# Moving three activation tiles by 384 or 256 bytes against their weight tiles, in a one-core block of recurrent, attention and feed-forward layers

## The chip, the cores and the metric

One NeuronCore of a Trainium2 chip runs the whole program. The metric is the device time of one execution in microseconds. For the kernel before, three runs gave 1909.07, 1909.23 and 1911.52 us, a median of 1909.23 us.

## What is computed

A batch of one sequence with 256 tokens and 1024 channels goes through two blocks. All tensors are float32. The first block has a recurrent layer, a gated feed-forward network, an attention layer and a second network; the second block has two modulated layers, each of which feeds one large projection into three branches (attention, a delta-rule recurrence, a gated linear attention) and merges them.

```
def swiglu_layer(x, norm_g, w_gate_up, w_down):
    h = rmsnorm(x, norm_g)
    g, u = jnp.split(h @ w_gate_up, 2, axis=-1)
    return x + (jax.nn.silu(g) * u) @ w_down

def second_block(...):
    for l in range(DEPTH):
        h = _rms_norm(x, norm_pre[l]) * (1 + scale[:, None, :]) + shift[:, None, :]
        p = h @ w_in[l]
        ...
        merged = (jax.nn.sigmoid(gate_a) * o_mla + jax.nn.sigmoid(gate_b) * o_rwkv
                  + jax.nn.sigmoid(gate_c) * o_gla)
        y = merged @ w_out[l]
        x = x + gate[:, None, :] * _rms_norm(y, norm_post[l])
```

What matters here are the products of activations with large weight matrices: `h @ w_in`, `h @ w_gate_up`, the product with `w_down`, the projections to queries, keys and values, and the output projections.

## The kernel before

Channels lie on the 128 partitions and tokens along the free axis (T = 256), so a tensor of 1024 channels is a tile of 8 rows (`DK`) of 256 float32 in each partition, 1024 bytes a row.

A large product is made in three passes. Weights and activations are each split into a rounded part (type float32r) and the rounded rest; the product is the sum of high by high, high by low and low by high. Each pass over 128 channels is one matmul that streams 256 columns, with a weight load of 128 columns ahead of it. Such a matmul, rounded, 128 by 256, is called a rounded matmul below; the program has 11,112 of them, and some fp32 matmuls between them.

Weights come in units of 1024 x 128 (`UNIT`, 4096 bytes in a partition). SyncE loads one into one of five raw slots (`UNIT_RAW`), ScalarE (L726) or VectorE (L721) writes its high part into one of three slots (`UNIT_HIGH`), and VectorE writes the low part over the raw one (`UNIT_LOW`, L737). TensorE then works through the unit with 24 rounded matmuls: in `multiply_unit` (L712, where the weights are the loaded operand and the activation streams; L701, the `by_token` form, where the activation is the loaded operand and the weights stream) or, for the first two units of a layer, in `first_units_by_pieces` (L671). The activation is `HX`, the layer's input, in most of these products; it is `H_PARTS` in the projections to queries, keys and values, and another tile (`DIRECT_HIGH`, `OM_HIGH`, `R_HIGH`, `OG_HIGH`, `M_HIGH` and others) in the output projections.

The feed-forward networks (`ffn_pe`, with `three_passes` at L1490, L1491 and L1492, and L1505 for the first piece) work in the same way with `H_PARTS` as the input of the up projection and `HIDDEN_PARTS`, the inner rows, as that of the down projection. Their weight parts are in `part_slots`. The up projection is a loop over 11 turns of two halves, 48 rounded matmuls a half; the down projection a loop over 4 turns of two halves, 66 rounded matmuls a half. Here ScalarE (L2396, L2428) and VectorE (L2316, L2324) split the weights, and VectorE evicts and gates the results (L2329 to L2346; L2346 writes the low part of the inner rows).

All tiles stand at addresses that are written out by hand. All weight tiles of these products begin at the same byte modulo 512, their rows are 512 or 1024 bytes, and those of the activations 1024. So the distance from a matmul's weight operand to its streamed operand, modulo 512, is the same for every matmul of a product. `LINE` (128 floats, 512 bytes) is the room in which a tile is shifted, and `X_SHIFT`, `H_SHIFT` and `HIDDEN_SHIFT` (L185) give the shift of the high and low tile in floats:

```
X_SHIFT, H_SHIFT, HIDDEN_SHIFT = (16, 16), (16, 16), (48, 48)
HX = [shaped(x_room[:, X_SHIFT[e] + e * DK * T:X_SHIFT[e] + (e + 1) * DK * T], (DK, T)) for e in range(2)]
om_at += (lent + X_SHIFT[0] - om_at) % 64
```

The first line is L185, the second L338, the third L390: `OM_HIGH` and `OM_LOW`, which feed one output projection in each layer of the second block, follow `X_SHIFT`, but modulo 64 floats (256 bytes).

The order of the work is the order in which it is written for each engine, with semaphores between the engines; no scheduler has a hand in it.

Of the kernel before, what the change touches and what calls it, by code (L numbers as in the profile page):

```python
# [163 lines left out]
def program(nc, A, out, stop=None):  # L164
    with ExitStack() as ctx:
# [16 lines left out]
        KD_ = FFN // P  # L182
        UNIT, RAWS, HIGHS = DK * P, 5, 3
        LINE = 128
        X_SHIFT, H_SHIFT, HIDDEN_SHIFT = (16, 16), (16, 16), (48, 48)  # L185
        WHOLE = 2 * KD_ * COLS + 2 * 2 * T + LINE
        SPLIT_AT, SPLIT = COMMON + WHOLE, 2 * 2 * DK * COLS + 2 * DK * T + 2 * KD_ * T + 2 * LINE
        psum = [ctx.enter_context(nc.psum_tensor(f"bank{i}", [P, 512], F32))[:, :] for i in range(8)]
# [3778 lines left out]
```

How the kernel before makes its waits and increments, by code:

```python
        def load_first_up(l):  # L564
            sp.wait_ge(unit_used.sem, last_split[l] + 1)
            for s in range(2):
                for to, frm in ffn_up[l].loads(s, WHOLE_UP[s]):
                    sp.dma_start(to, frm).then_inc(landed[s].sem, 16)
# [1 line left out]
        def load_up(l):  # L571
            job, turns = ffn_up[l], turns_before[l]
            with sp.Fori(1, UPS) as j:
                for s in range(2):
                    sp.wait_ge(lo_ready[s].sem, j + turns)
                    for to, frm in job.loads(j * 2 + s, WHOLE_UP[s]):
                        sp.dma_start(to, frm).then_inc(landed[s].sem, 16)
# [1 line left out]
        def load_down(l):  # L579
            job, turns = ffn_down[l], turns_before[l]
            for q in range(2):
                sp.wait_ge(lo_ready[q].sem, turns + UPS)
                for to, frm in job.loads(q, WHOLE_DOWN[q]):
                    sp.dma_start(to, frm).then_inc(landed[q].sem, 16)
            with sp.Fori(1, DK // 2) as j:
                for q in range(2):
                    sp.wait_ge(lo_ready[1].sem, j * 2 + (turns + UPS + q - 1))
                    for to, frm in job.loads(j * 2 + q, WHOLE_DOWN[q]):
                        sp.dma_start(to, frm).then_inc(landed[q].sem, 16)
# [46 lines left out]
        def load_units(job):  # L636
# [1 line left out]
                u = job.first + i  # L638
                if u >= RAWS:
                    sp.wait_ge(unit_used.sem, u - RAWS + 1)
                for to, frm in job.loads(i, UNIT_RAW[u % RAWS].rearrange("p (k c) -> p k c", k=job.kt)):
```

## Time and profile before

| | |
|---|---|
| median of three runs | 1909.23 us |
| the profiled execution, its own time | 1910.01 us |
| its span on the core | 1908.2 us |
| TensorE matmul busy | 1829.3 us, 96% |
| TensorE weight load busy | 1719.4 us, 90% |
| VectorE busy | 1367.7 us, 72% |
| ScalarE busy | 852.7 us, 45% |
| granted TensorE clock, mean | 0.992 |
| moved by DMA | 291.97 MB, 153 GB/s |

Busy time counts a matmul from its start to its modelled end, some 280 ns, while the next one begins some 115 ns after it: matmuls overlap in the pipeline. The pace is the distance from one start to the next. The profile's chain of waits, which goes back from the last instruction to what released each step, counts a matmul only until the next one starts, and so a merged piece of the chain (start, time, line, count) gives the pace as time divided by count.

### The profile page before, as it was taken

Reading aid. Unit: us, or ns where it says so; the run is one execution under the profiler, and the core shown is the slowest. Engines: PE = TensorE matmul, PEld = TensorE weight load, DVE = VectorE, ACT = ScalarE, POOL = GpSimd, SP = SyncE. Lnnn points to the kernel's source line nnn. Section 1 sums busy time; section 2 is a strip of 40 time slices with the busy share of each in tenths; the row PEclk is TensorE's granted clock in tenths of the full one; section 3 lists DMA queues with packets and bytes.
Section 4 is the critical chain, followed back from the end, with each engine's and each line's share of the span. In section 5 each row is a group of like instructions: output and inputs, shape, how many; then the busy total and the mean of one; then the engine's idle time right before and its main releaser. Section 6 shows DMA issues by size and latency. Waiting matters only on the chain.

```text
span 1908.2 us, 43158 instructions
## 1 busy us (share of the span) xinstructions
PE 1829.3 (96%) x18639; PEld 1719.4 (90%) x18639; DVE 1367.7 (72%) x1735; ACT 852.7 (45%) x1263; POOL 88.3 (5%) x131
## 2 busy tenths in 40 slices
PE   7999999999899999999998999997999998999999
PEld 7987999998699999998997899997998997889988
DVE  8996688758748876776886469666776886458755
ACT  5572534345634333226764233254216774334154
POOL 2000000010500000002000000000002000000000
PEclk9999999999999999999999999999999999999999
DMA  8555477975437795663560145554663561145544
GB/s 226 146 144 155 122 243 261 272 204 161 117 100 248 263 275 139 163 181 92 160 172 4 54 117 166 144 150 127 156 183 94 155 172 32 38 110 158 164 123 132
DMA packets 473230, 291.97 MB, mean 153 GB/s; under 512 B 26775, under 2 KB 467580, under 8 KB 472872
## 3 DMA queue, kind: packets, MB, share of 16 engines
q1 hardware_dynamic: 466720, 262.13, 48.6%
q0 software_dynamic: 5312, 25.32, 3.5%
q10 hardware_dynamic: 1032, 2.11, 0.4%
q8 instruction: 128, 2.10, 0.4%
q14 instruction: 38, 0.31, 0.0%
HBM read 287.95 MB, written 1.05 MB: 151 GB/s over the span
## 4 chain that ended last, share of the span: by engine, by line
PE 80%; DVE 12%; ACT 4%; issue 2%; DMA 2%; ACTq 0%; DVEq 0%; POOL 0%; SPq 0%
PE bank L712 39%; PE bank L1490 6%; PE bank L1491 6%; PE bank L1492 6%; DVE rounded L737 3%; PE bank L953 3%; PE bank L671 3%; PE bank L701 2%; PE bank L1678 1%; PE bank L1691 1%; PE bank L945 1%; DVE rounded L721 1%; ACT rounded L726 1%; PE bank L1659 1%; PE bank L794 1%
## 5 line engine op out<-in xcount | busy, mean ns | idle before, releaser
L712 PE MATMUL bank<-rounded 128*128 128x256 f32 x6504 | 789.9, 282 | 12.2 <-DVE rounded L737 9.9
L712 PEld LDWEIGHTS bank<-rounded 128*128 128x128 f32 x6504 | 771.0, 188 | 27.3 <-DVE rounded L737 14.5
L737 DVE TENSOR_TENSOR rounded<-arena,rounded 128x1024 fp32r<-128x1024 f32 x331 | 400.2, 1216 | 87.1 <-ACT rounded L726 78.1
L726 ACT ACTIVATE rounded<-arena 128x1024 fp32r<-128x1024 f32 x216 | 227.1, 1058 | 163.2 <-PE bank L712 108.6
L1490 PE MATMUL bank<-parts 128*128 128x256 f32 x1024 | 286.7, 280 | 2.3 <-DVE parts L2324 2.3
L1491 PE MATMUL bank<-parts 128*128 128x256 f32 x1024 | 285.4, 279 | 0.0
L1492 PE MATMUL bank<-parts 128*128 128x256 f32 x1024 | 285.2, 279 | 0.0
L1490 PEld LDWEIGHTS bank<-parts 128*128 128x128 f32 x1024 | 192.7, 188 | 3.5 <-issue 1.6
L1492 PEld LDWEIGHTS bank<-parts 128*128 128x128 f32 x1024 | 192.2, 188 | 0.0
L1491 PEld LDWEIGHTS bank<-parts 128*128 128x128 f32 x1024 | 191.9, 187 | 0.1
L777 ACT ACTIVATE arena<-bank 128x512 f32<-128x512 f32 x90 | 53.2, 596 | 238.6 <-PE bank L712 227.0
L2396 ACT ACTIVATE parts<-whole 128x2048 fp32r<-128x2048 f32 x44 | 84.3, 1917 | 127.4 <-PE bank L1492 104.1
L721 DVE CAST rounded<-arena 128x1024 fp32r<-128x1024 f32 (+1 forms) x115 | 78.2, 680 | 67.0 <-PE bank L712 41.9
L2316 DVE TENSOR_TENSOR parts<-whole,parts 128x2048 fp32r<-128x2048 f32 x44 | 100.8, 2292 | 19.2 <-ACT parts L2396 18.5
L953 PE MATMUL bank<-common,arena 128*128 128x128 f32 x519 | 77.8, 285 | 14.6 <-DMA common<-in_const 7.1
L953 PEld LDWEIGHTS bank<-common,arena 128*128 128x128 f32 x519 | 58.4, 144 | 25.0 <-DMA common<-in_const 7.1
L2324 DVE TENSOR_TENSOR parts<-whole,parts 128x1408 fp32r<-128x1408 f32 x32 | 52.0, 1625 | 36.5 <-ACT parts L2428 36.1
L2428 ACT ACTIVATE parts<-whole 128x1408 fp32r<-128x1408 f32 x32 | 44.2, 1381 | 66.2 <-PE bank L1492 52.9
L2713 DVE COPY arena<-bank 128x256 f32<-128x256 f32 (+2 forms) x64 | 33.6, 525 | 42.7 <-PE bank L1678 19.3
L712 PE MATMUL bank<-common,arena 128*128 128x256 f32 x256 | 59.8, 385 | 0.0
L701 PE MATMUL bank<-rounded 128*128 128x256 f32 x480 | 58.5, 282 | 0.7 <-DVE rounded L737 0.7
L701 PEld LDWEIGHTS bank<-rounded 128*128 128x128 f32 x480 | 56.6, 189 | 2.2 <-DVE rounded L737 1.1
(409 smaller groups left out, 2369.6 us busy)
## 6 DMA issues: line engine op xcount, KB each, us to landing
arena<-in_w_in SPq DMA_DIRECT2D x190, 512.0 KB, 3.8
whole<-in_ffn_w_gate_up SPq DMA_DIRECT2D x44, 1024.0 KB, 5.1
arena<-in_ada_w POOLq DMA_DIRECT2D x32, 768.0 KB, 6.3
whole<-in_ffn_w_down SPq DMA_DIRECT2D x16, 1408.0 KB, 6.9
arena<-in_rec_w_in SPq DMA_DIRECT2D x36, 512.0 KB, 3.7
arena<-in_att_w_qkv SPq DMA_DIRECT2D x24, 512.0 KB, 3.9
arena<-in_rec_w_out SPq DMA_DIRECT2D x16, 512.0 KB, 3.9
arena<-in_mla_w_o SPq DMA_DIRECT2D x16, 512.0 KB, 4.0
```

The lines of the kernel that those rows point to most:

```text
L671: last = pe.matmul(psum[s][:, i * T:i * T + T], w[a][:, kk, :], job.rhs[b][:, kk, :], start=(i, kk, a, b) == (0, 0, 0, 0), stop=kk == job. ...
L701: last = pe.matmul(psum[s][:, t * COLS:t * COLS + COLS], x[b][:, at + k, t * P:t * P + P], w[a][:, k, n * COLS:n * COLS + COLS], start=beg ...
L712: last = pe.matmul(psum[s][0:c, m % 2 * T:m % 2 * T + T], w[a][:, k, cols], x[b][:, k, :], start=(k, a, b) == (0, 0, 0), stop=k == job.kt ...
L721: write(high_view(job_of[u], u), raw_view(job_of[u], u, UNIT_RAW)).then_inc(done.sem, 1)
L726: high_parts(act, lambda to, frm: act.activation(to, frm, ACT.Copy), high_by_act[0].pop(0), unit_high_s)
L737: dve.tensor_tensor(raw_view(job_of[u], u, UNIT_LOW), raw, high_view(job_of[u], u).bitcast(F32), ALU.subtract)\
L953: last = pe.transpose(bank[:, n * P:n * P + P], x, ident)
L1490: pe.matmul(bank, w_hi, x_hi, start=start and k == 0, stop=False)
L1491: pe.matmul(bank, w_hi, x_lo, start=False, stop=False)
L1492: last = pe.matmul(bank, w_lo, x_hi, start=False, stop=stop and k == n - 1)
L2316: dve.tensor_tensor(UP_W[s][1], WHOLE_UP[s], UP_W[s][0].bitcast(F32), ALU.subtract)\
L2396: act.activation(UP_W[s][0], WHOLE_UP[s], ACT.Copy)\
```

## The change

One line is different. The three shifts become 112 floats, 448 bytes. No instruction is added, removed or moved on any engine; DMA transfers, waits and shapes are the same.

```diff
-        X_SHIFT, H_SHIFT, HIDDEN_SHIFT = (16, 16), (16, 16), (48, 48)
+        X_SHIFT, H_SHIFT, HIDDEN_SHIFT = (112, 112), (112, 112), (112, 112)
```

What this does to the distance of the streamed operand behind the weight operand, in bytes modulo 512, worked out from the addresses of all rounded matmuls:

| product | lines | before | after | rounded matmuls |
|---|---|---|---|---|
| `HX` and `H_PARTS` streamed | 671, 712 | 64 | 448 | 5,160 |
| up projections (`H_PARTS`) | 1490 to 1492, 1505 | 64 | 448 | 2,112 |
| down projections (`HIDDEN_PARTS`) | 1490 to 1492 | 192 | 448 | 1,056 |
| `HX` and `H_PARTS` as loaded operand | 701 | 448 | 64 | 576 |
| `OM_HIGH`, `OM_LOW` streamed | 712 | 320 | 192 | 384 |
| all others | 671, 701, 712 | 0 to 448 | the same | 1,824 |

In the fourth row the roles are exchanged, so a tile that begins 64 bytes behind the weights makes the weights begin 448 bytes behind it. The fifth row follows from the 256 bytes of L390. fp32 matmuls and the transposes keep their addresses.

## Rows read from the trace of the kernel before

**Rows 1.** The page, parts 1 and 2: busy time; granted TensorE clock by slice.
```profile
PE 1829.3 (96%) x18639; PEld 1719.4 (90%) x18639; DVE 1367.7 (72%) x1735; ACT 852.7 (45%) x1263; POOL 88.3 (5%) x131
PEclk9999999999999999999999999999999999999999
```
**Rows 2.** The page, part 4 (chain by engine), and the chain's shares by line.
```profile
PE 80%; DVE 12%; ACT 4%; issue 2%; DMA 2%; ACTq 0%; DVEq 0%; POOL 0%; SPq 0%
by line: PE bank L712 39.4%; PE bank L1490 6.0%; PE bank L1491 5.9%; PE bank L1492 5.8%; DVE rounded L737 2.9%; PE bank L953 2.6%; PE bank L671 2.5%; issue 2.2%; PE bank L701 2.1%; PE bank L1678 1.3%; PE bank L1691 1.2%; PE bank L945 1.1%;
```
**Rows 3.** Groups by form, PE: line, engine, operands, shape, count | busy us, mean ns | idle.
```profile
L712 PE MATMUL bank<-rounded 128*128 128x256 f32 x6432 | 781.7, 282 | 12.2 <-DVE rounded L737 9.9 <-ACT arena L777 1.6 <-ACT common L3323 0.6
L1490 PE MATMUL bank<-parts 128*128 128x256 f32 x1024 | 286.7, 280 | 2.3 <-DVE parts L2324 2.3
...
L701 PE MATMUL bank<-rounded 128*128 128x256 f32 x480 | 58.5, 282 | 0.7 <-DVE rounded L737 0.7
```
**Rows 4.** The chain in order of time, pieces of L712: start us, us, what, count.
```profile
943.43 31.09 PE bank L712 x264
...
1341.83 19.04 PE bank L712 x168
...
1386.43 42.41 PE bank L712 x360
```
**Rows 5.** Windows, all engines: two in up projections, the last in a down projection.
```profile
268.50:346.50 78.00, 78.00 (x664) 78.00 (x664) 64.96 (x56) 29.72 (x21) 3.70 (x7) 1.00 0.77 257
590.50:679.50 89.00, 89.00 (x758) 89.00 (x757) 74.09 (x64) 33.78 (x24) 4.23 (x8) 1.00 0.77 258
686.00:740.00 54.00, 54.00 (x479) 54.00 (x478) 36.87 (x31) 19.56 (x16) 2.11 (x4) 1.00 0.95 267
```
The columns of rows 5 are the stretch, its length, then busy time and count of PE, PEld, DVE, ACT and POOL, the granted clock, the busy share of the DMA engines and GB/s.

**Rows 6.** Timeline: the first and the last merged row of rounded matmuls.
```profile
18.15 0.84 PE L671 MATMUL bank<-rounded 128*128 128x256 f32 x5
...
1898.35 1.35 PE L712 MATMUL bank<-rounded 128*128 128x256 f32 x10
```
**Rows 7.** Windows, PE alone: L712 on OM_HIGH and OM_LOW.
```profile
912.00:933.00 21.00, 21.00 (x180) 1.00 0.61 174
```
**Rows 8.** The chain in order of time, pieces of L701.
```profile
853.33 2.75 PE bank L701 x24
859.77 2.75 PE bank L701 x24
...
1434.39 2.75 PE bank L701 x24
1440.82 2.83 PE bank L701 x24
```
**Rows 9.** Windows, PE alone: the three long stretches of L701.
```profile
472.00:487.00 15.00, 15.00 (x130) 1.00 0.30 88
1197.00:1206.00 9.00, 9.00 (x82) 1.00 0.70 184
1776.00:1786.00 10.00, 10.00 (x87) 1.00 0.67 179
```
**Rows 10.** Waits of PE: line, releaser, us in total, times, longest.
```profile
PE bank L712 <- DVE rounded L737: 10.6, 13, 1.4
```
**Rows 11.** The chain in order of time, in the first down projection.
```profile
359.35 10.15 DMA whole<-in_ffn_w_down
```
**Rows 12.** Groups by form, DVE: the two halves of a weight unit.
```profile
L737 DVE TENSOR_TENSOR rounded<-arena,rounded 128x1024 fp32r<-128x1024 f32 x328 | 399.3, 1224 | 87.0 <-ACT rounded L726 78.1
...
L721 DVE CAST rounded<-arena 128x1024 fp32r<-128x1024 f32 x112 | 77.5, 692 | 66.3 <-PE bank L712 41.2 <-PE bank L671 9.1 <-ACT arena L3859 8.6
```
**Rows 13.** Groups, DVE, from 590 to 680 us (an up projection).
```profile
L2346 DVE TENSOR_TENSOR parts<-apart,parts 128x512 fp32r<-128x512 f32 x8 | 5.6, 694 | 0.3
L2340 DVE TENSOR_TENSOR apart<-apart,common 128x512 f32<-128x512 f32 x8 | 5.5, 693 | 0.3
```

## The prediction

> **What bounds the kernel now.** I read first the page's shares: TensorE works in 1829.3 of 1908.2 us and its clock is granted in full in every slice, so it is on the upper of its two levels, 2.4 GHz, from end to end [rows 1]. Then the chain of waits: 80% of it is TensorE, and L712 alone is 39.4%, the three lines 1490 to 1492 another 17.7% [rows 2]. So what bounds the time is the pace at which one rounded 128x256 matmul follows another. The groups by form show nearly all of them in L712, L1490 to L1492 and L701, every one shown as some 280 ns long [rows 3]; that is the length of one in a pipeline and hides the pace. The pace stands in the chain's merged pieces, time divided by count. There the same instruction of the same line has two paces: 31.09 us / 264 = 117.8 ns and 42.41 / 360 = 117.8 ns, but 19.04 / 168 = 113.3 ns [rows 4]. Nothing released either, and the clock was the same. I take 4.5 ns as the price of the slow pace.
>
> The pace does not wander. A stretch keeps the one that it took within its first few matmuls, for as long as the stretch lasts: the windows of the feed-forward networks show it over 78 and 89 us (a window also counts the two or three matmuls that began just before it, so 89.00 / (758 - 2.5) = 117.8 ns), and over 54 us at the other pace (54.00 / (479 - 2.4) = 113.3 ns) [rows 5]. These two stretches also tell what the pace has to do with the change. They are the same three lines, the same loop body and the same weight tiles. The slow ones are the up projection, whose moving operand (H_PARTS) lies 64 bytes behind the weights modulo 512; the fast one is the down projection, whose moving operand (HIDDEN_PARTS) lies 192 bytes behind. The Trainium skill, TensorE: Matmul & The Clock Gate, Part 2, says in its step on LDWEIGHTS that weights and moving operand come through two independent read ports, so that loading weights takes nothing from a running matmul. This trace does not bear that out as it stands, with 113.3 beside 117.8 ns; what it would make of the change is the second rival.
>
> **What each place is worth, from the rows.** From the first rounded matmuls at 18.15 us to the last ten at 1898.35 there are 11,112 [rows 6]. Counted by the distance from one start to the next, with distances over 125 ns left out, the share at the fast pace is 13% of the 7,272 that go from 64 to 448, 68% of the 1,056 that go from 192 to 448 (57% of all that lie at 192), and none of the 384 of OM_HIGH, which go from 320 to 192 and run at 21.00 / (180 - 2.4) = 118 ns [rows 7].
>
> For 448 the trace has a stand-in. In L701 the layer's input is the weight operand and the weight tile streams, so there the moving operand lies 64 bytes ahead of the weights, which is 448 behind, modulo 512. Its separate pieces show both paces: 2.75 / 24 = 114.6 ns three times, which with a start of some 30 ns is the fast one, 2.83 / 24 = 118 ns for the slow one [rows 8]. Of three long stretches one is fast at 9.00 / (82 - 2.4) = 113.1 ns, and two are slow at 15.00 / (130 - 2.4) = 117.6 and 10.00 / (87 - 2.4) = 118.2 ns [rows 9]. That is 4 fast and 3 slow. Over all L701 matmuls at 448 it is 36%, because the longest stretch took the slow pace. The change swaps the two: 576 matmuls of L701 go from 448 to 64 (31% of these are fast now).
>
> **The sum.** No instruction, wait or transfer is added, removed or moved; only addresses change. Let p be the share at the fast pace at 448 after the change. The bounds of p are what the trace shows at the four places: none (320) and 68% (the down projection), and nothing excludes 100%, which the 54 us stretch reaches. Nearest is L701, with 36% by matmuls and 4 of 7 by stretches; starts at 192 look alike, with 57% by matmuls. What is short in L701 is long in L712, so I weight stretches more than matmuls and take p = 0.55.
>
> - 64 to 448: 7,272 x (0.55 - 0.13) = 3,054 more at the fast pace.
> - 192 to 448: 1,056 x (0.55 - 0.68) = 137 fewer.
> - 320 to 192: 384 x (0.57 - 0) = 219 more.
> - 448 to 64 in L701: 576 x (0.14 - 0.31) = 98 fewer (0.14 is the share over all 8,040 that lie at 64 now).
>
> Together 3,038 x 4.5 ns = 13.7 us of TensorE time. What of it reaches the end: L712 waits 10.6 us in all for the vector engine's halves of the weights [rows 10], some 1.4% of its time, and in the first down projection the chain runs through a 10.15 us load of weights [rows 11]. There a faster pace is lost in the wait behind it. I take 95%: 13.0 us. The cover elsewhere holds: a unit of 24 matmuls takes 24 x 117.8 = 2.83 us now and 2.72 then, against 1.22 us of L737 and 0.69 us of L721 on the vector engine, and in the up projection the vector engine is at 74.09 of 89.00 us, which becomes 87% [rows 5, 12]. Were that cover gone, the wait that comes next would be L712 on L737 again.
>
> The vector and scalar engines write the moved tiles. I cost that at nothing: L2346, which writes a moved tile, takes 694 ns and L2340, of the same shape with no such tile, 693 [rows 13]. A difference of a few ns would lie under the matmuls that these lines run beside.
>
> The profiled execution was 1910.0 us with a span of 1908.2; the median of the three runs is 1909.2, 0.8 us less. 1910.0 - 13.0 = 1897.0, against the median **1896 us**.
>
> Every tenth of p is worth (7,272 + 1,056) x 0.1 x 4.5 ns x 0.95 = 3.6 us, and the sum is zero at p = 0.185: there 7,272 x 0.055 = 400 and 219 are paid for by 523 in the down projections and 98 in L701. About 0.2%, or 3.8 us, is what a measurement of this kernel can tell from no change. So it is faster by more than that above p = 0.29 and slower by more than that below 0.08.
>
> **The rivals.**
>
> *The fast pace everywhere at 448* (p near 1). For it: the fast pieces of L701 lose some 30 ns in their first matmuls and then settle [rows 8], so a slow start at 448 need not last, and in a loop of hundreds there are many chances to slip. Against it: the 15 us in L701 that stayed slow from end to end [rows 9]. The time would be 1909.2 - 0.815 x 35.6 = 1880 us; at p = 0.9, 1884.
>
> *The place plays no part.* The paces would come from how each stretch happens to start, and each place in the program would keep its own. For it: L712 shows both paces at one and the same distance [rows 4]. Against it: 2,010 of 2,010 counted up-projection matmuls are slow and the second down projection is fast but for its beginning [rows 5], in the same lines. The time would be 1909. The page's two independent ports would make it come out so.
>
> *448 holds the slow pace.* At the start of the long stretches, the up projections above all, 448 lets the slow pace in as 64 and 320 do, and the down projections lose what 192 gave them. Place: L1490 to L1492 at 686 us and after. Price: with p = 0.05, (7,272 + 1,056) x (0.05 - 0.185) x 4.5 ns x 0.95 = 4.8 us, which is 1914 us. It decides below p = 0.185, and can be told from no change below 0.08. For it: of the three long stretches of L701 two are slow, the longest among them [rows 9], and the loops of the networks are longer still. Against it: four of all seven stretches at 448 are fast [rows 8, 9].
>
> *It does not do what it says.* OM_HIGH is aligned to 256 bytes and not to 512, so it lands at 192 and not 448; the term is in the sum, 0.9 us at most, and the forecast does not hang on it. That the remaining 1,824 matmuls, which keep their place, start in another phase can move the time by a microsecond either way.
>
> **How the numbers follow.** Chances: the forecast (p from 0.29 to 0.85) 0.60; fast everywhere 0.12; place plays no part, or p ends only just above its zero (0.185 to 0.29), 0.15; 448 holds the slow pace 0.13, of which 0.09 below p = 0.08. That gives faster 0.72, same 0.15 + 0.04 = 0.19, slower 0.09. The range runs from p = 0.9 (1884 us) to the point of no change (1909 us, p = 0.185), a little over both.
>
> **What would show it.** In the chain after, L712 pieces with 96 and more matmuls should mostly divide to 113 to 114 ns; in the windows of the up projections (89 us now) at least one should count about 113.3 ns a matmul and so end some 3 us sooner. The second down projection should be as fast as now, or slow at 117.8 ns and so some 2 us longer. L701's pieces should be slower, and L712 on OM_HIGH should show the fast pace in one of its two stretches. The forecast is wrong if all paces stand as before, if the up projections stay at 117.8 ns throughout, if a third pace shows up, or if matmuls get faster and the waits of L712 for L737 grow by as much.

## The result and the profile after

The changed kernel takes 1901.99 us in the median of 12 runs, the kernel before 1910.62 us in 12 runs beside it. The ratio is 0.9949, with a 95% interval of 0.9927 to 0.9971: faster by 0.5%, which is 9.7 us (the two medians lie 8.6 us apart). The profiled execution took 1903.7 us with a span of 1901.9, 6.3 us less than the profiled one of before.

The page after, busy time and the chain by engine, and below them the chain's shares by line:

```profile
PE 1820.5 (96%) x18639; PEld 1710.9 (90%) x18639; DVE 1366.7 (72%) x1735; ACT 852.7 (45%) x1263; POOL 88.6 (5%) x131
...
PE 74%; DVE 16%; ACT 5%; issue 3%; DMA 2%; ACTq 0%; DVEq 0%; POOL 0%; SPq 0%
```
```profile
by line: PE bank L712 34.7%; PE bank L1490 5.7%; PE bank L1491 5.6%; PE bank L1492 5.6%; DVE rounded L737 4.2%; issue 2.7%; PE bank L953 2.6%; PE bank L671 2.6%; PE bank L701 2.1%; DVE arena L1996 1.5%; ACT rounded L726 1.3%; PE bank L1678
```

The other engines' busy time is what it was. TensorE's share of the chain fell from 80 to 74%, L712's from 39.4 to 34.7%, and L737, which makes the low part of the weights, rose from 2.9 to 4.2% [rows 2]: a little of the path now runs through the vector engine. The chain in order of time, pieces of L712 after (start us, us, what, count):

```profile
757.93 19.04 PE bank L712 x168
...
940.22 31.09 PE bank L712 x264
...
1383.10 41.58 PE bank L712 x360
```

The first divides to 113.3 ns. The second is 117.8 ns to the digit, as in [rows 4] at 943.43. The third, 42.41 us before, is 115.5 ns: part of it changed pace, and the experiments below show which part. The windows of the networks, all engines: two in the first up projection, one in the second, and the second down projection last:

```profile
227.00:287.00 60.00, 60.00 (x512) 60.00 (x511) 47.26 (x42) 25.86 (x19) 2.65 (x5) 1.00 0.68 230
290.00:331.00 41.00, 41.00 (x364) 41.00 (x363) 35.08 (x30) 16.03 (x12) 2.12 (x4) 1.00 0.77 264
587.50:679.00 91.50, 91.50 (x779) 91.50 (x778) 75.51 (x67) 35.23 (x26) 4.24 (x8) 1.00 0.79 260
683.00:738.00 55.00, 55.00 (x469) 55.00 (x468) 36.02 (x30) 19.52 (x16) 2.12 (x4) 1.00 0.93 262
```

Less the 2.4 matmuls that began before a window, these are 117.7, 113.4, 117.8 and 117.9 ns. One stretch of the first up projection is fast; the second up projection is as slow as before, and the second down projection, fast in [rows 5], is now slow. OM_HIGH shows the fast pace in one of its two stretches (21.20 / 185.6 = 114.2 ns, and 118.2 ns), and of the four pieces of L701 in [rows 8] one stood at 2.83 us before and two do now:

```profile
908.80:930.00 21.20, 21.20 (x188) 1.00 0.64 181
1487.00:1508.00 21.00, 21.00 (x180) 1.00 0.63 175
```
```profile
852.41 2.75 PE bank L701 x24
858.85 2.83 PE bank L701 x24
...
1430.22 2.75 PE bank L701 x24
1436.66 2.83 PE bank L701 x24
```

Two covers that the prediction named: L712 waits 11.8 us for L737 in place of 10.6 [rows 10], and L2346, which writes a moved tile, keeps its 693 to 694 ns [rows 13].

```profile
PE bank L712 <- DVE rounded L737: 11.8, 16, 1.5
```

**Where the 6.3 us of the two profiles came from.** The time between starts, added up by product: the streamed layer input gave 7.1 us, the up projections 1.9, OM_HIGH 0.8 and the attention's projections 0.4; the down projections took 2.3, L701 0.8 and the unmoved products 0.8. The same time can be split by the length of the distances, each counted against 117.8 ns. Those up to 125 ns, which are the pace, gave 6.4 us. Of the longer ones, 25 fewer of the input's fell where the lower clock was granted, which gave 2.1 us. The others, at the full clock, are waits and breaks between products, and they took 2.1 us more than before.

### The profile page after: what moved, and what is told of

It reads as the page before. It is cut to its first block, busy times and chain, and to the rows that moved or that the text cites. A ratio compares the mean times of both kernels' runs of the same rounds, so it can differ in the third digit from the quotient of the medians.

```text
span 1901.9 us, 43158 instructions
## 1 busy us (share of the span) xinstructions
PE 1820.5 (96%) x18639; PEld 1710.9 (90%) x18639; DVE 1366.7 (72%) x1735; ACT 852.7 (45%) x1263; POOL 88.6 (5%) x131
## 4 chain that ended last, share of the span: by engine, by line
PE 74%; DVE 16%; ACT 5%; issue 3%; DMA 2%; ACTq 0%; DVEq 0%; POOL 0%; SPq 0%
PE bank L712 35%; PE bank L1490 6%; PE bank L1491 6%; PE bank L1492 6%; DVE rounded L737 4%; PE bank L953 3%; PE bank L671 3%; PE bank L701 2%; DVE arena L1996 1%; ACT rounded L726 1%; PE bank L1678 1%; PE bank L1691 1%; DVE rounded L721 1%; PE bank L945 1%; PE bank L1659 1%
## 5 line engine op out<-in xcount | busy, mean ns | idle before, releaser
L712 PE MATMUL bank<-rounded 128*128 128x256 f32 x6504 | 780.9, 281 | 13.4 <-DVE rounded L737 11.1
L712 PEld LDWEIGHTS bank<-rounded 128*128 128x128 f32 x6504 | 761.9, 188 | 28.9 <-DVE rounded L737 15.6
L737 DVE TENSOR_TENSOR rounded<-arena,rounded 128x1024 fp32r<-128x1024 f32 x331 | 399.8, 1216 | 85.1 <-ACT rounded L726 76.1
L712 PE MATMUL bank<-common,arena 128*128 128x256 f32 x256 | 59.8, 385 | 0.0
L701 PE MATMUL bank<-rounded 128*128 128x256 f32 x480 | 59.1, 282 | 0.6 <-DVE rounded L737 0.5
L701 PEld LDWEIGHTS bank<-rounded 128*128 128x128 f32 x480 | 57.1, 188 | 2.2 <-DVE rounded L737 1.2
```

The lines of the kernel that those rows point to most:

```text
L701: last = pe.matmul(psum[s][:, t * COLS:t * COLS + COLS], x[b][:, at + k, t * P:t * P + P], w[a][:, k, n * COLS:n * COLS + COLS], start=beg ...
L712: last = pe.matmul(psum[s][0:c, m % 2 * T:m % 2 * T + T], w[a][:, k, cols], x[b][:, k, :], start=(k, a, b) == (0, 0, 0), stop=k == job.kt ...
L737: dve.tensor_tensor(raw_view(job_of[u], u, UNIT_LOW), raw, high_view(job_of[u], u).bitcast(F32), ALU.subtract)\
```

## The experiments

The table gives for each profile the share at the fast pace, counted from one start to the next (up to 115 ns fast, 115 to 125 ns slow, longer distances left out). "Input" is the 4,776 matmuls of L671 and L712 that stream `HX`.

| kernel | distance of input, up, down | input | up | down | OM_HIGH |
|---|---|---|---|---|---|
| before | 64, 64, 192 | 20% | 0% | 68% | 0% |
| before again | 64, 64, 192 | 8% | 0% | 12% | 0% |
| after | 448, 448, 448 | 52% | 25% | 25% | 49% |
| after again | 448, 448, 448 | 63% | 7% | 71% | 1% |
| x_only | 448, 64, 192 | 58% | 0% | 77% | 1% |
| h_only | 64, 448, 192 | 20% | 4% | 80% | 0% |
| keep_hidden | 448, 448, 192 | 63% | 34% | 31% | 49% |
| all_192 | 192, 192, 192 | 48% | 2% | 24% | 37% |
| all_320 | 320, 320, 320 | 15% | 18% | 0% | 0% |
| all_128 | 128, 128, 128 | no such two paces | | | |
| all_224 | 224, 224, 224 | no such two paces | | | |
| fresh_448 | 448, 448, 448 | 55% | 87% | 52% | 1% |
| fresh_64 | 64, 64, 192 | 17% | 84% | 81% | 0% |
| two_distances | 192 and 448 | 67% | 2% | 40% | 1% |

**Both kernels a second time** (`before_again`, `after_again`), with no edit.

> The kernel before, unchanged, for a second profile. Theory (the distance between the operands sets how likely a stretch is to take the fast pace, and each stretch draws its pace anew in each execution): at 64 the draw is nearly always slow, so both up projections count 117.8 ns a matmul again, all 2,112 of them; at 192 it is mixed, so the down projections may come out otherwise than in the first profile, between 30% and 90% fast. Rival (the pace belongs to the place in the program and the way each stretch starts, the distance plays no part): the first down projection mixed and the second fast as in the first profile, stretch by stretch. Time within 0.3% of 1910 us under both.

> The changed kernel, unchanged, for a second profile. Theory: stretches at 448 draw anew, so several long stretches that were slow in the first profile are fast here and the other way about, with 35 to 60% of the 8,328 matmuls at 448 fast; the time lies anywhere between 1892 and 1912 us. Rival (pace belongs to the place): the same stretches fast and slow as in the first profile, and the time within 0.3% of the first profile's 1903.7 us.

Windows, PE alone, of the second profile of the kernel before (two up projections, then the second down projection), and of the second profile of the changed one in the same order; the columns are the stretch, its length, busy time and count, the granted clock, the DMA engines' busy share and GB/s:

```profile
230.00:330.00 100.00, 100.00 (x851) 1.00 0.72 242
580.00:680.00 100.00, 100.00 (x851) 1.00 0.78 261
695.00:745.00 50.00, 50.00 (x427) 1.00 0.95 268
```
```profile
235.00:345.00 110.00, 110.00 (x937) 1.00 0.77 257
580.00:670.00 90.00, 90.00 (x767) 1.00 0.75 257
698.00:750.00 52.00, 52.00 (x461) 1.00 0.98 274
```

Before: the up projections are at 100 / 848.6 = 117.8 ns again. The second down projection, 54 us at 113.3 ns in [rows 5], is at 50 / 424.6 = 117.8 ns, in the same kernel at the same place. After: the stretch of the first up projection that was fast is slow here, and the second down projection goes the other way, 117.9 to 113.4 ns.

So some stretches draw their pace anew in each execution, as the theory had it; the down projections' 12% lies below the 30% that was expected, and at 448 46% of the moved matmuls are fast, within the 35 to 60% expected. Others do not draw: the piece of L712 with 264 matmuls at 31.09 us (943.43 before, 940.22 after) takes 31.09 us in both second profiles too. The two times, 1921.1 and 1920.8 us, lie outside what was expected. Of the 11.0 us by which the span of the kernel before is longer than in its first profile, 3.4 lie between the starts of its rounded matmuls, which were slower here, and 7.6 outside them. In the changed kernel the rounded matmuls took no longer (0.1 us less), and 16.8 us lie outside them. Where the clock was lower is told at the end of this document.

**One tile alone** (`x_only`, `h_only`, `keep_hidden`).

```diff
-        X_SHIFT, H_SHIFT, HIDDEN_SHIFT = (16, 16), (16, 16), (48, 48)
+        X_SHIFT, H_SHIFT, HIDDEN_SHIFT = (112, 112), (16, 16), (48, 48)
...
+        X_SHIFT, H_SHIFT, HIDDEN_SHIFT = (16, 16), (112, 112), (48, 48)
...
+        X_SHIFT, H_SHIFT, HIDDEN_SHIFT = (112, 112), (112, 112), (48, 48)
```

> Only X_SHIFT goes to 112 floats; H_SHIFT and HIDDEN_SHIFT stay. Theory: the 4,776 matmuls that stream the layer's input go from about 20% fast to about 50%, OM_HIGH from none to about half, the 384 of L701 that load it from 36% to about 14%: some 1,630 more at the fast pace, by 4.5 ns and 95% some 7 us, ratio 0.9963 (0.994 to 0.998). The up projections stay wholly at 117.8 ns, the down projections mixed to fast. Rival (distance plays no part): ratio 1.000. Second rival (all of the gain comes from the networks): ratio 1.000 here and the gain in the next run.

> Only H_SHIFT goes to 112 floats. Theory: the 2,112 matmuls of the up projections go from none fast to a mixed share (25% in the first profile after, between 10 and 60% by the long stretches they come in), the 384 of the attention's projections likewise, L701's 192 from 22% to none: some 500 more at the fast pace, 2 us, ratio 0.999 (0.9955 to 1.000). The layer's input stays at some 20%. Rival (distance plays no part): ratio 1.000 and the up projections slow throughout. Second rival (all gain from the networks): ratio 0.995.

> X_SHIFT and H_SHIFT at 112 floats, HIDDEN_SHIFT left at 48, so the down projections stay at 192. Theory (192 and 448 are alike, so the term for the down projections was no loss): ratio as the change itself, 0.995 (0.992 to 0.998), down projections mixed. Rival (moving the inner rows cost a microsecond or two): ratio 0.994. The two can hardly be told apart by time; the profile's share of the down projections is the test.

The layer's input alone: 1905.0 against 1912.5 us, ratio 0.9957 (0.9931 to 0.9983). The chain of `x_only`, pieces of L712 that stood at 117.1 and 117.8 ns before, and the windows of its two up projections and its second down projection:

```profile
755.19 19.04 PE bank L712 x168
...
1383.57 41.58 PE bank L712 x360
```
```profile
235.00:340.00 105.00, 105.00 (x894) 1.00 0.75 254
565.00:670.00 105.00, 105.00 (x894) 1.00 0.76 256
684.00:736.00 52.00, 52.00 (x461) 1.00 0.96 271
```

The 168 are at 113.3 ns and the 360 at 115.5 ns, as with the whole change, while the up projections stay at 105 / 891.6 = 117.8 ns. That is the theory's number (0.9963) and refutes both rivals. OM_HIGH, at 192 here too, stayed slow, so half for it was not to be relied on.

The network input alone: ratio 0.9988 (0.9959 to 1.0018), against 0.999 expected. The interval holds no change, and it excludes the 0.995 of the second rival. The share of the up projections, 4%, is below the 10% that was expected at the least; the windows of `h_only` show one of them slow from end to end, 105 / 891.6 = 117.8 ns:

```profile
565.00:670.00 105.00, 105.00 (x894) 1.00 0.77 259
```

The inner rows left at 192: ratio 0.9939 (0.9908 to 0.9971), which cannot be told from the change itself, as expected. Its second down projection was slow like that of the first profile after, and at 192, so nothing here shows 448 to be a worse place for it than 192.

**Other distances** (`all_192`, `all_320`, `all_128`, `all_224`, `two_distances`), with all three shifts at 48, 80, 32 and 56 floats, and at 48 for the high tiles with 112 for the low ones.

```diff
-        X_SHIFT, H_SHIFT, HIDDEN_SHIFT = (16, 16), (16, 16), (48, 48)
+        X_SHIFT, H_SHIFT, HIDDEN_SHIFT = (48, 48), (48, 48), (48, 48)
...
+        X_SHIFT, H_SHIFT, HIDDEN_SHIFT = (48, 112), (48, 112), (48, 112)
```

> All three shifts at 48 floats: streamed operands lie 192 bytes behind the weights, OM_HIGH too, and the 576 of L701 at 320. Theory (the distance sets the chance of the fast pace, 192 like 448): the layer's input comes out 40 to 65% fast, the up projections 5 to 40% (their long stretches start behind slow work), the down projections as before, L701 wholly slow. Some 2,000 more at the fast pace, ratio 0.996 (0.992 to 0.999). Rival (448 alone does it, by its mirror place to 64): the layer's input stays under 25% fast, ratio 1.000. Rival (distance plays no part): ratio 1.000.

> All three shifts at 80 floats: 320 bytes, where OM_HIGH had no fast matmul in either profile of before. Theory: none of the 8,328 streamed matmuls that move, and none of OM_HIGH, is at the fast pace, 117.8 ns throughout; L701 goes to 192 and is mixed, 20 to 80% fast. Beside a profile of before with equal time at the lower clock this is some 5 to 6 us more. Rival (pace belongs to the place and its start): the layer's input 10 to 20% fast and the second down projection fast, as before.

> All three shifts at 32 floats: 128 bytes; L701 and OM_HIGH at 384. Theory: the share lies between that of 64 (8 to 20%) and of 192 (12 to 80%), as the 128 matmuls that lie at 128 before suggest with 14%; a pace slower than 117.8 ns shows up, since those take 118 to 123. Rival (distance plays no part): 10 to 20% of the layer's input fast and no third pace.

> All three shifts at 56 floats: 224 bytes, not a multiple of 64; L701 at 288. Theory: the distance works in steps, not by whether it is a multiple of 64, so the share is like that of 192, 40 to 65% of the layer's input. Rival (steps of 64 bytes matter, a tile that straddles them streams slower): every moved matmul slower than 117.8 ns. The vector and scalar instructions that write the moved tiles keep their durations under both (L2346 some 694 ns).

> The high tiles at 48 floats and the low ones at 112, so a product alternates between 192 and 448 from pass to pass. Theory (192 and 448 are alike): the layer's input 40 to 65% fast, no new pace. Rival (a change of distance inside the stretch upsets a settled pace): under 25% fast or a third pace over 118 ns; or the other way, a stretch that starts slow slips into the fast pace and over 75% are fast.

At 192 the input is 48% fast and the ratio 0.997 (0.9953 to 0.9986), as expected. Two shares missed: the up projections have 2%, and L701, at 320, is not wholly slow (of 376 of its `HX` matmuls 37% are fast). At 320 the down projections are wholly slow, as expected and against the rival. But the input is 15% fast, which is the rival's figure (10 to 20%), and one long stretch of the up projections is fast, where the theory had none. Windows of `all_320`, the fast stretch and the one after it:

```profile
628.00:665.00 37.00, 37.00 (x328) 1.00 0.75 255
687.00:740.00 53.00, 53.00 (x452) 1.00 0.93 260
```

37 / 325.6 = 113.6 ns and 53 / 449.6 = 117.9 ns. So 320 can hold the fast pace too; in this one profile it took it less often than 448 did.

At 128 and 224 the pattern itself is another. The chain of `all_128`, and then of `all_224`:

```profile
1346.11 19.89 PE bank L712 x168
...
1392.06 42.59 PE bank L712 x360
...
1529.01 34.56 PE bank L712 x288
```
```profile
1531.62 34.30 PE bank L712 x288
```

These are 118.4, 118.3, 120.0 and 119.1 ns. The single distances scatter from 115 to 123 ns in place of standing at two values, with means of 119.0 and 118.2 ns for the input. Both means are above the slow pace at 64. The theory had expected 224 to be like 192: wrong, and so is its rival that every moved matmul would be slower than 117.8 ns, since single distances go down to 115. Expected for 128 was a pace over 117.8 ns, and it is there. L2346 keeps its 692 to 693 ns in both. That a matmul's pace follows the place of its operand, with nothing else changed, is shown by these two. `all_128` also shows that what counts is the place of the one operand against the other, and not that of the streamed tile alone: L701 and OM_HIGH lie at 384 there and scatter in the same way, with means of 118.7 and 118.6 ns (116.4 and 117.8 before), though in L701 the streamed tile, the weights, stands where it stood. The Trainium skill's sentence on two independent read ports (TensorE: Matmul & The Clock Gate, Part 2), by which loading weights takes nothing from a running matmul, is not borne out for these 256-column float32r streams, where the same instruction takes 113.3, 117.8, 119.1 or 120.0 ns on average with its operand at other bytes.

Changing the distance inside a product (192 for the high tile, 448 for the low) gives the input 67% fast and no new pace; it neither upsets a pace nor helps the up projections (2%).

**More starts** (`fresh_448`, `fresh_64`): one fp32 matmul ahead of each half of the up projections.

```diff
                 pe.wait_ge(lo_ready[s].sem, j + (turns + 1))
+                pe.matmul(psum[s][:, 0:P], ident, ones, start=True, stop=True)
                 for m in range(2):
```

> The changed kernel with one extra fp32 matmul (128 columns of ones, against the identity) ahead of each half of the up projections, into the bank that the half then starts over; 42 of them. Theory (the pace is drawn at a start and kept; 448 makes the fast draw likelier; the up projections stay slow because they have only some two to four starts each): with 42 starts the up projections come out 40 to 80% fast, against 25 and 7% in the two profiles of the change without the extra matmul. Rival (the loop itself, its load of the vector engine or of the DMA queues, keeps it slow): still under 25%. The extra matmuls cost some 0.2 us each, so the time is no test.

> The kernel before with the same extra fp32 matmul ahead of each half of the up projections. Theory: the starts are as many as in the run before this one, but at 64 a start is drawn slow in nearly all cases, so the up projections stay under 25% fast (0 and 0% in the two profiles of before, 8 to 20% in L712 at 64). Rival (starts alone decide, whatever the distance): as fast as at 448, 40 to 80%.

The up projections were 87% fast at 448, and 84% fast at 64. Windows of the second up projection, of `fresh_448` and of `fresh_64`:

```profile
600.00:650.00 50.00, 50.00 (x442) 1.00 0.75 257
```
```profile
600.00:650.00 50.00, 50.00 (x444) 1.00 0.74 250
```

With the extra matmuls counted in, these are 50 / 439.6 = 113.7 and 50 / 441.6 = 113.2 ns from one start to the next. The timeline of `fresh_64`, PE alone (start us, us, line, operation, tiles, shape, count): the end of one half, the extra matmul in its two passes, and the next half:

```profile
248.15 0.28 PE L1492 MATMUL bank<-parts 128*128 128x256 f32 x1
248.26 0.28 PE L1490 MATMUL bank<-parts 128*128 128x256 f32 x1
248.37 0.28 PE L1491 MATMUL bank<-parts 128*128 128x256 f32 x1
248.49 0.28 PE L1492 MATMUL bank<-parts 128*128 128x256 f32 x1
248.60 0.38 PE L1515 MATMUL bank<-common 128*128 128x128 f32 x2
248.74 0.36 PE L1490 MATMUL bank<-parts 128*128 128x256 f32 x1
248.94 0.28 PE L1491 MATMUL bank<-parts 128*128 128x256 f32 x1
249.05 0.28 PE L1492 MATMUL bank<-parts 128*128 128x256 f32 x1
249.17 0.28 PE L1490 MATMUL bank<-parts 128*128 128x256 f32 x1
```

The starts stand 0.11 to 0.12 us apart on both sides. The rival that the loop keeps the up projections slow falls at both distances. So does my theory in the form that it had: at 64 I expected under 25%. Behind the two passes of this fp32 matmul most halves of the up projections settle on 113.3 ns, at either distance; without it they begin at 117.8 ns and mostly stay there, also at either distance. So what stands ahead of a stretch can set its pace. The halves are not separate draws, though: in `fresh_64` the first three halves of both up projections are slow and all but one of the others fast. Each of the two kernels was profiled once.

**A change of distance without a start.** The start is not all, and the traces show that without a further run. In each layer of the second block TensorE passes from the layer's input to the unmoved tiles `CQ_HIGH` and `CQ_LOW`, 64 bytes behind the weights, inside one piece of L712 and without a pause. The piece of 360 above is one of them: some 190 matmuls of the input, then some 170 of unmoved tiles. Windows before and behind the passage in the changed kernel, and then in the kernel before, before the second passage and behind the first:

```profile
1384.00:1404.00 20.00, 20.00 (x179) 1.00 0.72 191
1406.00:1424.00 18.00, 18.00 (x155) 1.00 0.72 187
```
```profile
1388.00:1408.00 20.00, 20.00 (x172) 1.00 0.67 185
829.00:846.00 17.00, 17.00 (x152) 1.00 0.72 192
```

The changed kernel goes from 20 / 176.5 = 113.3 to 18 / 152.6 = 118.0 ns. It does so from one matmul to the next: the twelve distances ahead of the first matmul on the new tile are 113 or 114 ns, the twelve behind it 117 to 119. The same stands at both passages in all six profiles with the input at 448 (in `two_distances` at 192 and 448). Where the input lies at 64, 192 or 320, six profiles, the pace does not change there: it is slow on both sides, as at 20 / 169.6 = 117.9 ns, but for the first passage of the first profile before, from 64 to 64, which is fast ahead of it and stays fast behind it (17 / 149.5 = 113.7 ns). So a new distance alone, with no new start, changed the pace, and a new tile at the same distance did not. In the twelve profiles with two paces, no product settles from the fast pace into the slow one without a pause; each such turn falls where the tile changes. From slow to fast a product does turn by itself, 14 times in all.

So the start and the distance both set the pace. Over the whole program the input is fast in 8 to 20% of its matmuls at 64 and in 52 to 63% at 448.

The extra matmul costs about what it brings: from 243.07 us, where this half's first matmul starts, to 248.74, where the next one's does, a half takes 5.67 us, and 48 x 117.8 ns are 5.65. A cheaper way to make a start, such as fewer columns, was not tried, and whether the kind of the extra matmul, its place or its time does it was not taken apart.

## Why the prediction was right, and where it was not

- **Sign, size and the reason** held. 9.7 us against 13.0 forecast, 1902 us lies inside the range, whose ends are 1884 and 1909 us and a little over both. The gain comes from the pace of the rounded matmuls: the other engines' busy time stands and no instruction moved. That the size came so near is in part luck, since p was too high and so was the share that reaches the end, while the shares at the old places fell in the second profile.
- **64 to 448, streamed layer input.** p = 0.55 was taken; the profiles of the change show 52 and 63%, `x_only` 58%, from 20 and 8% at 64. This term is most of the gain, as `x_only` shows: 0.43% (0.17 to 0.69) beside 0.51%.
- **64 to 448, up projections.** This step failed: "I weight stretches more than matmuls and take p = 0.55" was one share for all products. The two profiles of the change show 25 and 7%, `h_only` 4%. Of the bounds at hand, none and 68%, the lower was the nearer one here. The loop itself does not force the slow pace: with an extra matmul ahead of each half it is 87% fast at the same distance (`fresh_448`), and 84% at 64. Why its own starts lead to the slow pace stays open.
- **192 to 448, down projections.** p fell from 68 to 25% in the first pair of profiles, a loss of 2.3 us; but the second pair goes from 12 to 71%. The term was read from one execution of a stretch that draws its pace anew, and has no settled sign. The same holds of the contrast on which the prediction rested the part of the distance, the slow up and the fast down projection [rows 5]: in the second profile of the same kernel the second down projection was slow.
- **320 to 192 and L701.** The signs held in the profile after, 0.8 us each way; OM_HIGH's share came out 49% once and 1% in the second profile, so it too varies.
- **p as a whole** was 0.40 in the first profile after and 0.46 in the second. By the prediction's own slope of 3.6 us a tenth, these give 7.6 and 9.8 us.
- **95% reaches the end.** This step failed too. Counted as above, the pace gave 6.4 us in the first pair of profiles and 16.3 us in the second, and the long distances at the full clock took back 2.1 and 6.2 us of it: 33 and 38%, not 5. The wait that the prediction named, L712 for L737, grew by 1.2 and 2.6 us; the rest are other waits and breaks between products. That the first pair kept 6.4 us all the same is luck with the clock, which gave 2.1. With 62 to 67% in place of 95% the prediction's 13.7 us would have become 8.5 to 9.2.
- **A stretch keeps its pace.** Within one product this held but for the 14 turns from slow to fast. Where the streamed tile changes the pace can change with it, as the piece of 360 shows, so a pace is not only taken at a start. Of the signs that the prediction named, the pieces of L712 with 96 and more matmuls failed: two of them divide to 113.3 ns in the profile after, as two did before, and not most.
- **The clock** was not at its upper level from end to end, as the prediction read it: its mean was 0.992, and 0.97 over the 50 us from 480 on.
- **The rivals.** "The fast pace everywhere" and "448 holds the slow pace" are refuted for the input and half true for the up projections, where the slow pace did hold. "The place plays no part" is refuted by `x_only`, by the scatter at 128 and 224 and by the turn inside the piece of 360, but its other half, that the way a stretch starts can set its pace whatever the distance, is what `fresh_64` shows.

What stays open is what inside the chip makes a start or a distance fast or slow. That the weight load and the stream get in each other's way at one distance and not at another is a possible story, and no run here shows where.

## What to carry to other kernels

A line that is always "busy" can still run at two paces: divide the chain's pieces by their counts before believing that a matmul stream is at its limit. If the streamed and the loaded operand have a fixed distance modulo 512 bytes, try a few odd multiples of 64 bytes, avoid 128 and 224, and judge them by the share of matmuls at the fast pace in two profiles, which tells more than one time. Look also at what stands ahead of a long run of matmuls, since its start can set the pace of hundreds, and at runs that pass without a pause to a tile at another distance. And do not count a gain in pace in full: here a third or more of it went into the waits behind it.

## What the runs showed of the hardware that was not expected

A pace that is kept for so long was not expected: each up projection of `x_only` holds 117.8 ns over the 891 matmuls of its window, through 18 halves, with no distance over 125 ns in the first window and one, of 140 ns, in the second.

The spread of single times, 1895.8 to 1915.8 us for the changed kernel, goes with the clock: the three of its twelve runs over 1909 us were granted 0.982 to 0.989 in the mean, the other nine 0.991 to 0.996. Windows over the attention layer, all engines, of the kernel before in its first profile, then of the changed kernel in its first profile and in its second:

```profile
480.00:530.00 50.00, 43.33 (x331) 34.03 (x329) 33.44 (x76) 28.78 (x87) 24.01 (x32) 0.97 0.36 99
```
```profile
480.00:530.00 50.00, 42.83 (x308) 32.76 (x308) 30.95 (x76) 29.20 (x87) 24.08 (x32) 0.93 0.35 96
```
```profile
480.00:540.00 60.00, 55.25 (x298) 41.53 (x298) 31.57 (x74) 26.81 (x84) 24.07 (x32) 0.66 0.29 80
```

The granted clock is the mean of the two levels, 2.4 and 1.2 GHz: 0.93 in the changed kernel's first profile and 0.66 in its second, in the same kernel, for the same work of some 300 matmuls, ten microseconds longer. The second execution had more matmuls at the fast pace (46 against 40%) and still a span of 1918.6 against 1901.9 us. In this stretch TensorE is not continuously busy, 42.83 of 50 us in the first profile; why the lower level lasts longer in some executions no run here tells. It happened with the kernel before as well, whose second profile took 1921.1 us and was granted 0.77 over the 50 us from 480 on.
